# A transformer block kernel on one core: the token factor of three norms moved from the products' input to their results, and one unused group of products left out

## The chip, the cores and the metric

The kernel is one program on one core of one Trainium2 chip. The metric is the time of one execution on the device, in microseconds (us). The core has a matrix engine (TensorE, PE in the profile; its weight loads are listed apart as PEld), VectorE (DVE), ScalarE (ACT), GpSimd (POOL) and SyncE (SP), which here only issues transfers. Each engine works through its own list of instructions in order, and the lists meet only at semaphores. Matmul results go to eight banks of PSUM (`pb0` to `pb7`, 128 x 512 floats each), from where DVE or ACT must fetch them before the bank is used again.

## The reference, cut to what matters

Two blocks follow each other over 512 tokens of 1024 features, all in float32. The change is in the second one:

```python
def rms_norm(x, w):
    xf = x.astype(jnp.float32)
    y = xf * lax.rsqrt(jnp.mean(xf * xf, axis=-1, keepdims=True) + EPS)
    return (y * w.astype(jnp.float32)).astype(x.dtype)

def swiglu(x, w_gate, w_up, w_down):
    return (jax.nn.silu(x @ w_gate) * (x @ w_up)) @ w_down

def second_block(x, ...):
    x = x + 0.5 * swiglu(rms_norm(x, ffn1_norm[l]), ffn1_w_gate[l], ffn1_w_up[l], ffn1_w_down[l])
    h = rms_norm(x, mix_norm[l])
    proj = h @ w_in[l]
    qkv_a, z_a, a_a, b_a, qkv_b = jnp.split(proj, split_at, axis=-1)
    o_a = gdn_mixer(qkv_a, z_a, a_a, b_a, conv_w[l], a_log[l], dt_bias[l], gdn_norm_w[l])
    o_b = dilated_mixer(qkv_b, q_norm_w[l], k_norm_w[l], rel_bias)
    x = x + jnp.concatenate([o_a, o_b], axis=-1) @ w_out[l]
    x = x + 0.5 * swiglu(rms_norm(x, ffn2_norm[l]), ffn2_w_gate[l], ffn2_w_up[l], ffn2_w_down[l])
    x = rms_norm(x, final_norm[l])
```

A root-mean-square norm multiplies each feature by a weight and each token by one factor, 1/sqrt(mean of squares + EPS). That factor is the same for all features of the token, so it may also be multiplied onto a product's result.

## The kernel before, in words

Activations lie with features across the 128 partitions and the 512 tokens along them, as eight tiles of 128 x 512 (`KC` = 8) in `xT`. A group of products is eight matmuls of 128 x 128 weights with these eight tiles, summed in one bank. Weights of 1 MB (`pair`, two groups) are streamed by SP into a ring of three slots (L400); PE signals `slot_free` when it begins a slot.

A norm (`rms`, numbered 0 to 3) goes over four engines. ACT squares the tiles (L1276), DVE adds the squares (`add_square`, L1820, 128 x 512 each), PE sums them over the partitions by one matmul with ones (L852), DVE scales and adds EPS (L1824), ACT takes the root (L1278), DVE the reciprocal (L1826); the result `rs` holds the token's factor in every partition. Then DVE multiplies each tile by the weight and by `rs` in one instruction (L1829) and counts `xn_ready` up; the products of the next stage wait for tile after tile.

The feed-forward (`feed_forward`, twice) has 22 halves (`half`): 16 matmuls into two banks, gate and up (L863); ACT takes the Silu of the gate bank (L1283), DVE multiplies it by the up bank (L1834). Three pairs of banks take turns. Then eight groups of 22 matmuls go down (L888), and DVE adds half of each result to `xT` (L1848).

Between the two feed-forwards stand 30 groups (`linear`, L535, `N_H` = 30) that make queries, keys, values and gates of two attention parts, in two banks by turns. The 30th has the same weights as the 29th (gates) and nothing reads it. ACT copies each result out of its bank (L1299). Beside this, DVE runs a convolution of five taps over 12 of the groups (`convolve`, L1870 and four of L1875), ACT takes its Silu (L1303), and the first 16 groups are normed by head: ACT squares (L1309), PE sums (L907), DVE scales (L1904), ACT takes the root of eight sums at once (L1313), DVE the reciprocal and the multiplication (`apply_norm`, L1886, L1890). The groups of values (16 to 19) are convolved in the turns 16 to 19. Behind the groups a short chain over DVE (from L1910), ACT and PE prepares the gates; then come 32 heads of attention, the chunked recurrence, the output product (`project`, L1066; DVE adds it to `xT`, L2072), norm 2 and the second feed-forward, and norm 3, whose result is stored.

While norm 0 begins, POOL still scales and shifts the token-major copy of the first block's result, tile by tile (`scale_rows`, L432 and L434). The order of all work is the order in which the code lists it; no scheduler moves anything.

## Time and profile before

| | us |
|---|---|
| median of 3 runs | 3819.41 (3816.04 to 3820.52) |
| profiled execution, its own time | 3819.16 |
| its span | 3817.6 |
| PE busy | 3498.3 (92%) |
| DVE, ACT, POOL busy | 1159.3, 757.9, 177.0 |
| granted PE clock, mean | 0.95 of full |

The second block begins at about 2204 us of the span. A row of the timeline gives the start and the duration in us, engine, line, operation and tiles; in brackets stands the idle time of the engine ahead of it and who ended it. The granted clock 1.00 is 2.4 GHz and 0.50 is 1.2 GHz. Matmuls in float32 leave two records each and are pipelined, so a row with x160 is 80 matmuls.

### The profile page before, as it was taken

How to read it: one execution, taken by the hardware profiler on the slowest of the kernel's cores; microseconds unless marked ns; L12 is line 12 of the kernel's file. 1: busy time of each engine (PE TensorE's matmuls, PEld its weight loads, DVE VectorE, ACT ScalarE, POOL GpSimd, SP SyncE). 2: the span in 40 equal slices, each digit the busy share in tenths (PEclk: the TensorE clock that was granted, in tenths of full speed). 3: DMA queues.
4: the chain of work that ended last, by engine and by line, in shares of the span. 5: the costliest groups of instructions: out<-in, count | busy, mean ns of one | idle time of the engine just before them, and what ended most of it. 6: DMA issues, size and time to landing. Idle time of an engine off the chain costs nothing. (4 is left out here: it accounts for less than half of the span.)

```text
span 3817.6 us, 47479 instructions
## 1 busy us (share of the span) xinstructions
PE 3498.3 (92%) x15780; PEld 1803.3 (47%) x15780; DVE 1159.3 (30%) x2400; ACT 757.9 (20%) x1418; POOL 177.0 (5%) x169
## 2 busy tenths in 40 slices
PE   8998998899969989997999679999998788899998
PEld 5445444555544454445555334444344577444443
DVE  1564112322333751113332320000446555410001
ACT  1134112223221151102222220000123422100000
POOL 1000002100020000003000110000000000000000
PEclk9999999899979999998999889999999887999999
DMA  7112223898231103234986212235121000122221
GB/s 280 56 45 78 77 77 132 324 389 353 77 130 66 56 23 112 76 133 153 420 336 268 81 57 77 77 83 143 67 76 54 1 0 0 44 77 77 77 77 66
DMA packets 79142, 457.64 MB, mean 120 GB/s; under 512 B 12160, under 2 KB 12296, under 8 KB 32112
## 3 DMA queue, kind: packets, MB, share of 16 engines
q1 hardware_dynamic: 42912, 310.40, 21.6%
q0 software_dynamic: 19776, 112.50, 8.3%
q10 hardware_dynamic: 16272, 32.43, 2.5%
q8 instruction: 100, 1.64, 0.2%
q14 instruction: 82, 0.67, 0.1%
HBM read 416.23 MB, written 39.06 MB: 119 GB/s over the span
## 5 line engine op out<-in xcount | busy, mean ns | idle before, releaser
L779 PE MATMUL pb<-arena,xT 128*64 x1984 | 445.6, 383 | 16.4 <-DVE streamed L1699 5.9
L779 PE MATMUL pb<-streamed,xT 128*64 128x256 f32 x1984 | 445.6, 383 | 0.0
L535 PE MATMUL pb<-xT,streamed 128*128 128x512 f32 x832 | 369.4, 603 | 0.0
L779 PEld LDWEIGHTS pb<-arena,xT 128*64 128x64 f32 x1984 | 267.8, 138 | 162.4 <-issue 31.6
L704 PE MATMUL pb<-xT,streamed 128*128 128x512 f32 x768 | 335.3, 595 | 2.6 <-ACT arena L1193 2.6
L888 PE MATMUL pb<-arena,streamed 128*128 128x512 f32 x704 | 306.4, 598 | 8.9 <-DMA streamed<-in_w_tail 7.2
L863 PE MATMUL pb<-xtok,streamed 128*128 128x512 f32 x704 | 305.0, 596 | 5.8 <-DVE xtok L1829 5.8
L863 PE MATMUL pb<-arena,streamed 128*128 128x512 f32 x704 | 304.2, 595 | 5.8 <-DVE arena L1829 5.8
L779 PEld LDWEIGHTS pb<-streamed,xT 128*64 128x64 f32 x1984 | 267.9, 138 | 0.0
L535 PEld LDWEIGHTS pb<-xT,streamed 128*128 128x128 f32 x832 | 159.9, 193 | 201.5 <-issue 201.4
L704 PEld LDWEIGHTS pb<-xT,streamed 128*128 128x128 f32 x768 | 146.4, 191 | 186.6 <-issue 186.6
L803 PE MATMUL pb<-arena,am 128*64 x496 | 224.6, 595 | 5.7 <-DVE streamed L1745 5.7
L803 PE MATMUL pb<-streamed,am 128*64 128x512 f32 x496 | 224.6, 595 | 0.0
L888 PEld LDWEIGHTS pb<-arena,streamed 128*128 128x128 f32 x704 | 134.7, 192 | 180.7 <-issue 171.8
L863 PEld LDWEIGHTS pb<-xtok,streamed 128*128 128x128 f32 x704 | 134.6, 191 | 176.1 <-issue 174.6
L863 PEld LDWEIGHTS pb<-arena,streamed 128*128 128x128 f32 x704 | 134.4, 191 | 176.3 <-issue 175.0
L535 PE MATMUL pb<-xtok,streamed 128*128 128x512 f32 x480 | 211.8, 599 | 5.8 <-DVE xtok L1829 5.8
L1834 DVE TENSOR_TENSOR arena<-pb,arena 128x512 f32 (+1 forms) x44 | 30.4, 692 | 572.5 <-ACT arena L1283 572.5
L714 PE MATMUL pb<-arena,streamed 128*128 x384 | 168.7, 592 | 0.0
L1571 DVE TENSOR_TENSOR arena<-pb,arena 128x512 f32<-128x512 f32 x48 | 33.2, 692 | 421.3 <-PE pb L714 421.3
L535 PEld LDWEIGHTS pb<-xtok,streamed 128*128 128x128 f32 x480 | 92.2, 192 | 122.8 <-issue 121.2
L1215 ACT ACTIVATE streamed<-arena 128x2048 f32 x62 | 118.5, 1912 | 155.2 <-issue 121.9
(359 smaller groups left out, 3756.8 us busy)
## 6 DMA issues: line engine op xcount, KB each, us to landing
arena<-in_w_moe SPq DMA_DIRECT2D x128, 1024.0 KB, 11.7
streamed<-in_w_tail SPq DMA_DIRECT2D x87, 1024.0 KB, 4.8
streamed<-in_w_layer SPq DMA_DIRECT2D x78, 1024.0 KB, 4.9
arena<-in_w_moe POOLq DMA_DIRECT2D x64, 1024.0 KB, 9.7
ys_dram<-am ACTq DMA_DIRECT2D x120, 128.0 KB, 6.5
xT<-xs_dram ACTq DMA_DIRECT2D x26, 512.0 KB, 8.2
xs_dram<-lnw POOLq DMA_DIRECT2D x16, 512.0 KB, 20.5
lnw<-in_ln_par POOLq DMA_DIRECT2D x4, 1024.0 KB, 5.3
```

What stands on the lines that cost most here:

```text
L535: last = mm(pb[bank][:, 0:cols], unit(w, u, k), rhs[:, k * cols:(k + 1) * cols], start=(k == 0), stop=(k == KC - 1))
L704: last = mm(pb[2 + d % 2][:], unit(w, u6 % 2, k), grp(xT, k), start=(k == 0), stop=(k == KC - 1))
L714: last = mm(pb[4 + e][:], unit(w, ub % 2, e * 4 + k), grp(big, n * 4 + k), start=(k == 0), stop=(k == 3))
L779: last = mm(pb[m][r0:r0 + MOE_BLOCK, 0:FW], rows, w, start=(k == 0), stop=(k == KC - 1))
L803: last = mm(pb[2 + b % 2][r0:r0 + MOE_BLOCK, 0:DW], hT[:, h0:h0 + MOE_BLOCK], w, start=(k == 0), stop=(k == 3))
L863: last = mm(pb[3 * u + s][:], unit(w, u, k), xn[:, k * S:(k + 1) * S], start=(k == 0), stop=(k == KC - 1))
L888: last = mm(pb[6 + g][:], unit(w, u % 2, c % KC), grp(big, c), start=(c == 0), stop=(c == FC - 1))
L1215: fn(cut(w1_relay, D_EXP - FW), cut(arena[:, bass.ds(values[0], KC * D_EXP)], D_EXP)[:, :, FW:D_EXP], ACT.Copy).then_inc(w1_relayed, 1)
L1571: v.tensor_tensor(tmp[d % 2], pb[4 + d % 2][:], relu2[d % 2], ALU.mult).then_inc(br_free, 1)
L1834: v.tensor_tensor(grp(big, f), pb[3 + s][:], sgl[s], ALU.mult).then_inc(ff_free, 1)
```

## The change

The weighting by the norm's weight (`weigh`) and the token's factor (`row_scale`) become two functions for the norms 0, 1 and 2; norm 3 stays as it was. The products read tiles that are only weighted. For norm 0 the weighings stand ahead of the adds of squares; for the norms 1 and 2 each tile is weighed as soon as its sum is in `xT`. PE's matmul of the sum stands behind the first half of products or the first group. The factor is multiplied in elsewhere: onto the gate bank, into `sgl`, ahead of the Silu; onto the down products' results, together with the 0.5; and onto each result of the 29 groups, where DVE takes over the fetching from PSUM that was ACT's. The input of the second feed-forward lies in `sr` and no more in `xtok`. The four groups of values are convolved in the turns 18, 20, 22 and 24 (`V_AT`), and the last eight `apply_norm` of DVE stand one in each turn from 21 on in place of behind the loop.

```diff
-H_Q, H_K, H_SQ, H_SK, H_V, H_Z, H_SV, H_AB, N_H = 0, 4, 8, 12, 16, 20, 24, 28, 30
+H_Q, H_K, H_SQ, H_SK, H_V, H_Z, H_SV, H_AB, N_H = 0, 4, 8, 12, 16, 20, 24, 28, 29
+V_AT = [18, 20, 22, 24]
...
-        xns = [sr[:, 0:KC * S], xtok[:, :], xtok[:, :], xtok[:, :]]
+        xns = [sr[:, 0:KC * S], xtok[:, :], sr[:, 0:KC * S], xtok[:, :]]
... (tensor engine)
                 half(pair(j0), 0, 0, True)
+                rms(2 * n)
...
-            rms(0)
             feed_forward(0, 0)
-            rms(1)
             pe.wait_ge(rel_copied, 2)
             for g in range(N_H):
                 linear(pair(34 + g // 2), g % 2, xns[1], DEPTH * LIN_LAYER + g, g % 2, norm=1 if g == 0 else None)
+                if g == 0:
+                    rms(1)
...
-            rms(2)
             feed_forward(1, 53)
... (scalar engine)
-                    act.wait_ge(ff_ready, n * FC + f + 1)
-                    fn(sgl[s], pb[s][:], ACT.Silu).then_inc(ff_silu, 1)
+                    act.wait_ge(ff_scaled, n * FC + f + 1)
+                    fn(sgl[s], sgl[s], ACT.Silu).then_inc(ff_silu, 1)
...
-                act.wait_ge(lin_ready, DEPTH * LIN_LAYER + g + 1)
-                fn(grp(big, g), pb[g % 2][:], ACT.Copy).then_inc(lin_free, 1)
-                if g - 2 in CONV_GROUPS:
-                    c = CONV_GROUPS.index(g - 2)
+                done = g - 2 if g - 2 < H_SQ else H_V + V_AT.index(g - 2) if g - 2 in V_AT else -1
+                if done >= 0:
+                    c = CONV_GROUPS.index(done)
                     act.wait_ge(conv_ready, c + 1)
-                    fn(grp(big, g - 2), ctmp[c % 2], ACT.Silu).then_inc(conv_silu, 1)
+                    fn(grp(big, done), ctmp[c % 2], ACT.Silu).then_inc(conv_silu, 1)
                 c = g - 3
                 if 0 <= c < N_NORM:
+                    act.wait_ge(lin_free, DEPTH * LIN_LAYER + c + 1 + 2)
... (vector engine)
+            def weigh(m, k):
+                v.tensor_scalar(grp(xns[m], k), grp(xT, k), normw[:, m * KC + k:m * KC + k + 1], None, ALU.mult).then_inc(xn_ready, 1)
+            def row_scale(m):
                 dve.wait_ge(ss_ready, m + 1)
                 v.tensor_scalar(rs, pb[7][:], 1.0 / D, EPS, ALU.mult, ALU.add).then_inc(rvar, 1)
                 dve.wait_ge(rstd, m + 1)
                 v.reciprocal(rs, rs)
                 dve.drain()
...
                 def half(f, s):
+                    dve.wait_ge(ff_ready, n * FC + f + 1)
+                    v.tensor_tensor(sgl[s], pb[s][:], rs, ALU.mult).then_inc(ff_scaled, 1)
                     dve.wait_ge(ff_silu, n * FC + f + 1)
                     v.tensor_tensor(grp(big, f), pb[3 + s][:], sgl[s], ALU.mult).then_inc(ff_free, 1)
...
-                    x = grp(xT, d)
-                    v.scalar_tensor_tensor(out=x, in0=pb[6 + d % 2][:], scalar=0.5, in1=x, op0=ALU.mult, op1=ALU.add).then_inc(dn_free, 1)
+                    x, y = grp(xT, d), sgl[d % 3]
+                    v.scalar_tensor_tensor(out=y, in0=pb[6 + d % 2][:], scalar=0.5, in1=rs, op0=ALU.mult, op1=ALU.mult)
+                    dve.drain()
+                    v.tensor_tensor(x, x, y, ALU.add).then_inc(dn_free, 1)
+                    if n == 0:
+                        dve.drain()
+                        weigh(1, d)
...
+            dve.drain()
+            for k in range(KC):
+                weigh(0, k)
             for k in range(KC):
                 add_square(0, k)
-            rms(0)
+            row_scale(0)
...
-            for g in range(N_NORM + 5):
-                if g in CONV_GROUPS:
+            for g in range(N_H):
+                dve.wait_ge(lin_ready, DEPTH * LIN_LAYER + g + 1)
+                v.tensor_tensor(grp(big, g), pb[g % 2][:], rs, ALU.mult).then_inc(lin_free, 1)
+                dve.drain()
+                if g < H_SQ:
                     convolve(g)
+                elif g in V_AT:
+                    convolve(H_V + V_AT.index(g))
...
-            for c in range(8):
-                apply_norm(1, c)
-            dve.drain()
+                if g >= N_NORM + 5:
+                    apply_norm(1, g - N_NORM - 5)
+                    dve.drain()
...
                 v.tensor_tensor(x, x, pb[OUT_BANKS[d]][:], ALU.add).then_inc(lin_free, 1)
+                dve.drain()
+                weigh(2, d)
```

On PE, where the first block ends and the second begins, the list before reads so (L548 are the last transposes, L852 the matmul of the sum, L863 the first half of products; x7 means seven alike):

```order
L548 MATMUL pb3<-cst,xtok 128x128 x4
L590 REGISTER_ALU
L590 COMPARE_AND_BRANCH
L852 MATMUL pb7<-am,cst 128x512 [waits squares_summed,xT_rest,xT_ready]
L863 MATMUL pb0<-arena,streamed 128x512 [waits xn_ready,ff_free,weights_loaded0]
L863 MATMUL pb0<-arena,streamed 128x512 [waits xn_ready] x7
L863 MATMUL pb3<-arena,streamed 128x512 x8
L869 UNCONDITIONAL_BRANCH
```

And now, at the same place (L854 is the matmul of the sum, L865 the products):

```order
L592 REGISTER_ALU
L592 COMPARE_AND_BRANCH
L865 MATMUL pb0<-arena,streamed 128x512 [waits ff_free,weights_loaded0,xn_ready,xT_rest,xT_ready]
L865 MATMUL pb0<-arena,streamed 128x512 [waits xn_ready] x7
L865 MATMUL pb3<-arena,streamed 128x512 x8
L854 MATMUL pb7<-am,cst 128x512 [waits squares_summed]
L872 UNCONDITIONAL_BRANCH
```

The matmul of the sum has moved behind the sixteen products of the first half.

On DVE, at the same place, before (L1820 the adds, L1824 and L1826 the factor, L1829 the input):

```order
L1820 TENSOR_TENSOR am<-am,arena 128x512 [waits sq_ready,xT_ready]
L1820 TENSOR_TENSOR am<-am,arena 128x512 [waits sq_ready] x6
L1824 TENSOR_SCALAR arena<-pb7 128x512 [waits sums_ready]
L1826 RECIPROCAL arena<-arena 128x512 [waits rms_std]
L1829 SCALAR_TENSOR_TENSOR arena<-xT,normw,arena 128x512 x8
L1836 UNCONDITIONAL_BRANCH [waits rows_scaled]
```

And now (L1826 is the weighing, L1822 the adds, L1831 and L1833 the factor, L1845 the new scaling of a gate bank):

```order
L1826 TENSOR_SCALAR arena<-xT,normw 128x512 [waits xT_ready]
L1826 TENSOR_SCALAR arena<-xT,normw 128x512 x7
L1822 TENSOR_TENSOR am<-am,arena 128x512 [waits sq_ready] x7
L1831 TENSOR_SCALAR arena<-pb7 128x512 [waits sums_ready]
L1833 RECIPROCAL arena<-arena 128x512 [waits rms_std]
L1849 UNCONDITIONAL_BRANCH [waits rows_scaled]
L1849 ISA
L1845 TENSOR_TENSOR arena<-pb0,arena 128x512 [waits ff_ready]
```

Eight instructions that waited for the factor became eight ahead of the adds that wait only for `xT`.

On DVE in the groups, where one turn has both a convolution and a norm by head, before (L1870 and L1875 the convolution, L1886 and L1890 `apply_norm`, L1904 the next sum):

```order
L1870 TENSOR_SCALAR arena<-arena,conv_w 128x512 [waits conv_silu,lin_free]
L1875 SCALAR_TENSOR_TENSOR arena<-arena,conv_w 128x510
L1875 SCALAR_TENSOR_TENSOR arena<-arena,conv_w 128x511 x2
L1875 SCALAR_TENSOR_TENSOR arena<-arena,conv_w 128x510
L1886 RECIPROCAL am<-am 128x512
L1890 SCALAR_TENSOR_TENSOR arena<-arena,am 128x512
L1904 TENSOR_SCALAR am<-pb 128x512 [waits norm_sums]
```

And now, in turn 18 and at the start of turn 19 (L1917 fetches a result from PSUM, L1890 and L1895 are the convolution, L1906 and L1910 `apply_norm`, L1929 the next sum):

```order
L1917 TENSOR_TENSOR arena<-pb,arena 128x512 [waits lin_ready]
L1890 TENSOR_SCALAR arena<-arena,conv_w 128x512 [waits conv_silu]
L1895 SCALAR_TENSOR_TENSOR arena<-arena,conv_w 128x510
L1895 SCALAR_TENSOR_TENSOR arena<-arena,conv_w 128x511 x2
L1895 SCALAR_TENSOR_TENSOR arena<-arena,conv_w 128x510
L1906 RECIPROCAL am<-am 128x512
L1910 SCALAR_TENSOR_TENSOR arena<-arena,am 128x512
L1929 TENSOR_SCALAR am<-pb 128x512 [waits norm_sums]
L1917 TENSOR_TENSOR arena<-pb,arena 128x512 [waits lin_ready]
```

The fetch that frees PE's bank stands in DVE's list now, behind all that the turn before had to do.

## Rows read from the trace of the kernel before

**Rows 1.** The page, part 1: engine, busy us (share), instructions.
```profile
PE 3498.3 (92%) x15780; PEld 1803.3 (47%) x15780; DVE 1159.3 (30%) x2400; ACT 757.9 (20%) x1418; POOL 177.0 (5%) x169
```
**Rows 2.** Waits of PE from 2224 us on: total us, times, longest.
```profile
PE pb L852 <- DVE am L1820: 7.7, 3, 2.8
...
PE pb L535 <- DVE xtok L1829: 5.8, 1, 5.8
```
**Rows 3.** Timeline of norm one: start us, duration us, engine, line.
```profile
2202.76 1.37 DVE L1456 TENSOR_SCALAR xT<-pb,ln_T 128x128 f32<-128x128 f32 x4 [3.95 <-PE pb L548]
...
2216.43 2.05 PE L852 MATMUL pb<-am,cst 128*128 128x512 f32 x2 [14.07 <-DVE am L1820]
...
2223.33 5.39 DVE L1829 SCALAR_TENSOR_TENSOR arena<-xT,normw,arena 128x512 f32<-128x512 f32 x8
...
2224.23 20.99 PE L863 MATMUL pb<-arena,streamed 128*128 128x512 f32 x44 [5.75 <-DVE arena L1829]
...
2240.10 0.60 ACT L1283 ACTIVATE arena<-pb 128x512 f32<-128x512 f32 x1 [18.93 <-PE pb L863]
```
**Rows 4.** DVE's adds (ns, min/median/max) and POOL's last two scalings beside them.
```profile
L1820 DVE TENSOR_TENSOR am<-am,arena x7: 692/693/2661, 2206.0 to 2215.6; 128x512 f32<-128x512 f32 x7
...
2207.05 2.80 POOL L432 TENSOR_TENSOR xtok<-xtok,lnw 128x1024 f32<-128x1024 f32 x1
...
2209.99 2.61 POOL L434 TENSOR_TENSOR xtok<-xtok,lnw 128x1024 f32<-128x1024 f32 x1
```
**Rows 5.** Groups of instructions by line: busy us, mean ns.
```profile
L1834 DVE TENSOR_TENSOR arena<-pb,arena 128x512 f32 (+1 forms) x44 | 30.4, 692 | 572.5 <-ACT arena L1283 572.5
...
L1870 DVE TENSOR_SCALAR arena<-arena,conv_w 128x512 f32<-128x512 f32 x12 | 5.8, 484 | 33.2 <-ACT arena L1303 20.8 <-ACT arena L1299 12.4
```
**Rows 6.** Timeline of norm two.
```profile
2694.00 0.69 DVE L1848 SCALAR_TENSOR_TENSOR xT<-pb,xT 128x512 f32<-128x512 f32 x1 [17.41 <-PE pb L888]
...
2703.26 27.26 PE L535 MATMUL pb<-xtok,streamed 128*128 128x512 f32 x56 [5.76 <-DVE xtok L1829]
```
**Rows 7.** Stages: window, its length, PE, PEld, DVE, ACT, POOL busy, clock, DMA.
```profile
2533.50:2535.00 1.50, 1.50 (x3) 0.68 (x2) 0.00 (x0) 0.00 (x0) 0.99 (x1) 0.50 0.29 38
...
2708.50:2709.40 0.90, 0.90 (x3) 0.41 (x2) 0.00 (x0) 0.00 (x0) 0.00 (x0) 0.57 1.03 437
...
3346.00:3347.60 1.60, 1.60 (x4) 0.57 (x3) 0.82 (x2) 0.00 (x0) 0.00 (x0) 0.51 0.81 323
...
3647.20:3649.00 1.80, 0.10 (x1) 0.00 (x0) 0.69 (x1) 1.65 (x2) 0.00 (x0) 1.00 0.00 0
```
**Rows 8.** Timeline of the groups: DVE's steps, then PE's, then what follows them.
```profile
2757.52 0.49 DVE L1870 TENSOR_SCALAR arena<-arena,conv_w 128x512 f32<-128x512 f32 x1 [3.34 <-ACT arena L1303]
...
2761.23 0.69 DVE L1904 TENSOR_SCALAR am<-pb 128x512 f32<-128x512 f32 x1
...
2816.65 3.35 DVE L1886 RECIPROCAL am<-am 128x512 f32<-128x512 f32 x1 [20.17 <-ACT am L1313]
...
2821.46 3.34 DVE L1886 RECIPROCAL am<-am 128x512 f32<-128x512 f32 x1
...
2787.86 7.03 PE L535 MATMUL pb<-xtok,streamed 128*128 128x512 f32 x16
...
2795.59 7.03 PE L535 MATMUL pb<-xtok,streamed 128*128 128x512 f32 x16
...
2857.39 68.83 PE L535 MATMUL pb<-xtok,streamed 128*128 128x512 f32 x160
...
2928.06 0.29 DVE L1910 COPY ab<-pb 128x128 f32<-128x128 f32 x1 [17.62 <-PE pb L913]
```
**Rows 9.** Timeline of norm three.
```profile
3333.08 0.69 DVE L2072 TENSOR_TENSOR xT<-xT,pb 128x512 f32<-128x512 f32 x1 [1.96 <-PE pb L1066]
...
3342.32 17.86 PE L863 MATMUL pb<-xtok,streamed 128*128 128x512 f32 x35 [5.75 <-DVE xtok L1829]
```
**Rows 10.** Timeline at the end of the first feed-forward's halves.
```profile
2529.88 1.88 PE L877 MATMUL pb<-arena,rel_b 32*8 32x512 f32 x4 [1.41 <-DVE arena L1834]
```

More of the change, by code:

```diff
@@ L292, in two_blocks @@
             sem(n) for n in ("sq_ready", "sq_used", "squares_summed", "sums_ready", "rms_var", "rms_std", "xn_ready"))
-        ff_ready, ff_silu, ff_free = sem("ff_ready"), sem("ff_silu"), sem("ff_free")
+        ff_ready, ff_scaled, ff_silu, ff_free = sem("ff_ready"), sem("ff_scaled"), sem("ff_silu"), sem("ff_free")
         dn_ready, dn_free = sem("down_ready"), sem("down_free")
@@ L1820, in add_square @@
                     v.tensor_tensor(sq_sum, sq_sum, sq2[k % 2], ALU.add).then_inc(sq_summed if k == KC - 1 else sq_used, 1)
-            def rms(m):
+            def weigh(m, k):
+                v.tensor_scalar(grp(xns[m], k), grp(xT, k), normw[:, m * KC + k:m * KC + k + 1], None, ALU.mult).then_inc(xn_ready, 1)
+            def row_scale(m):
                 dve.wait_ge(ss_ready, m + 1)
@@ L1827, in rms @@
                 dve.drain()
+            def rms(m):
+                row_scale(m)
                 for k in range(KC):
@@ L1853, in _ @@
             dve.wait_ge(xT_ready, 4 * KC + 1)
+            dve.drain()
+            for k in range(KC):
+                weigh(0, k)
             for k in range(KC):
                 add_square(0, k)
-            rms(0)
+            row_scale(0)
             dve.wait_ge(tok_done, 2 * DEPTH + 1)
             feed_forward(0)
-            rms(1)
+            row_scale(1)
             dve.wait_ge(rel_stored, 16)
@@ L1865, in convolve @@
                 x, y = grp(big, g), ctmp[c % 2]
-                dve.wait_ge(lin_free, DEPTH * LIN_LAYER + g + 1 + 2)
                 if c >= 2:
@@ L1892, in apply_norm @@
                     last.then_inc(n_done, 1)
-            for g in range(N_NORM + 5):
-                if g in CONV_GROUPS:
+            for g in range(N_H):
[3 more added lines that the diff above has]
+                if g < H_SQ:
                     convolve(g)
+                elif g in V_AT:
+                    convolve(H_V + V_AT.index(g))
                 c = g - 5
-                if c >= 0:
+                if 0 <= c < N_NORM:
                     if c >= 8:
@@ L2075, in _ @@
             add_square(2, KC - 1)
-            rms(2)
+            row_scale(2)
             feed_forward(1)
```

## The prediction

> **What bounds the kernel now.** I read the page first: TensorE (PE) is busy for 92% of the span [rows 1], so time can only be taken out of matmuls, out of the gaps between them, or out of stretches in which its clock is low. I then read the table of waits for the part behind the first 2224 us [rows 2] and looked up its large entries in the timeline: the three norms that the change touches are gaps in which PE waits for a chain on VectorE (DVE) and ScalarE (ACT). Last I read the same stretches in the table of stages, for the granted clock. I call the norms one (ahead of the first feed-forward), two (ahead of the 30 groups of products) and three (ahead of the second feed-forward). All three are short, so everything below is worked out from starts and ends in the timeline.
>
> In norm one the input is whole at 2204.13 (DVE L1456 from 2202.76 for 1.37), the sum of squares goes to PE at 2216.43, and the first product starts at 2224.23 [rows 3]. In norm two the last product is taken from PSUM at 2694.00 and the next one starts at 2703.26 [rows 6]; in norm three it is 3333.08 and 3342.32 [rows 9]. Now the products need only the weighted input (x times the norm's weight). The factor of the token, rs, is needed where a result leaves PSUM.
>
> **Units.** A group of eight matmuls takes 6.87 us at full clock (160 records, two a matmul, in 68.83 us), so one matmul 0.86; two products' starts lie 7.73 apart where one matmul of a sum stands between them [rows 8], which is 6.87 + 0.86 again. A DVE instruction with 512 columns from PSUM takes 0.69, the same times one number a row from SBUF to SBUF 0.48 [rows 5]; a drain adds about 0.08 (the step of 4.81 below holds instructions of 3.35, 0.69 and 0.69, together 4.73).
>
> **Norm one.** Eight weighings now stand ahead of the adds of squares. If nothing held them, the first would end at about 2204.9 and PE start there, 19.3 us earlier; in that place GpSimd (POOL) still runs its row scaling, until 2209.99 + 2.61 = 2212.60. The adds of before show what this does: their median is 693 ns, the longest took 2661 ns, and between two POOL instructions just one of them came through [rows 4]. No weighing ran beside POOL before, so its cost is unknown: between 0.48, as alone, and one for each POOL instruction, as the adds. I take the second: at 0.48 against 0.69 it moves elements faster than an add does, so it uses at least as much of the way to SBUF. Then weighings end at about 2205.0, 2207.7, 2210.4 and 2213.1, and the other four by 2214.7; PE does three matmuls in the holes and goes on without a stop from 2213.15. Thirteen of the half's sixteen matmuls are left, 11.2 us, and 2.0 to 2.8 more at low clock (below): it ends at 2226.4 to 2227.1. The seven adds, 0.78 each, end by 2220.2, so the matmul of the sum follows at once, 0.86, and the second half starts at about 2227.6. Before, it started with ACT's first Silu, 2240.0 [rows 3]. **Minus 12.4**; if nothing holds the weighings, minus 18.0 (first half 2205.0 to 2221.1, sum to 2222.0).
>
> The Trainium skill bears on the choice. Its page SBUF — State Buffer, section Who interferes with whom, says that GpSimd and VectorE share a pair of SBUF ports under an exclusive lock, taken for a whole instruction, by VectorE instructions with two SBUF inputs and also by tensor_scalar in its two-port mode; the trace agrees for the first kind, with the 2661 ns, and shows nothing of the second. By that rule the term is the minus 12.4, and by the reading that a single tensor input stays clear of POOL it is the minus 18.0.
>
> The old chain, matmul of the sum to first product (2216.43 + 2.05 to 2223.33 + 0.75, so 4.9 us until rs is there and 0.75 for a multiplication), now runs beside the second half of products. The first result waits for it until about 2232.6, which costs nothing: three pairs of banks are free, and the fourth half starts at 2227.6 + 27.5 = 2255.
>
> **Ends of both feed-forwards.** 22 halves of 13.7 us each get one more DVE multiplication (0.69 and about 0.06 to hand over), hidden but for the last, where PE waits for the chain Silu, multiplication [rows 10]: now scaling, Silu, multiplication. **Plus 0.75, twice.** The downward products get a second instruction and drain a group (0.77), hidden under 18.9 us but at the last: at the end of the first it is part of norm two, at the end of the kernel **plus 0.77**.
>
> **Norm two.** Last product out at 2694.00, 0.69, drain, add 0.69 to 2695.46, and PE goes on at about 2695.6: the weighings 0 to 6 are long done, and the eighth (0.5 more) is needed only 6 us later. **Minus 7.7**. The matmul of the sum no longer stands in a gap: **plus 0.86**.
>
> **The clock.** After each of the old gaps the granted clock was 0.5 (1.2 GHz of 2.4) for some microseconds: until 2708.8 and until 3347.6 [rows 7]. By the sum, norm two's groups cost 2926.22 - 2703.26 = 222.96 where 30 x 6.87 + 16 x 0.86 = 219.8 were due: 3.2 us; norm three likewise 2.8. The gaps shrink from 2.4 + 5.8 us to 1.8 and 0.9. In the gap of 1.7 us at the end of the second feed-forward, and behind it, the clock stayed at 1.0; behind the like gap of the first (1.4 us, then two short matmuls that use eight columns of the array) a stretch from 2533.5 stood at 0.5 [rows 7]. I take no fall: **minus 3.2 and minus 2.8**. If it falls after all, between 0 and 2.8 comes back at a place; I price it at two thirds of norm three's, 1.9, since the gaps are shorter.
>
> **The groups.** Group 30, which nothing reads, goes: **minus 6.87** on PE. ACT's copy out of PSUM becomes a DVE multiplication. Is DVE in time? Steps from starts in rows 8: a convolution 2761.23 - 2757.52 = 3.71; reciprocal, multiplication and the next sum's scaling 2821.46 - 2816.65 = 4.81; the new copy 0.77. So the turns are 0.77 + 3.71 (groups 0 to 7, and + 0.61 from 5), 0.77 + 4.81 = 5.58 (13 to 20) and, with one of the four convolutions (18, 20), 9.29; from 21 on 0.77 + 4.19, and 8.67 at 22 and 24. PE needs 7.73 a group until 19, 6.87 after. A copy may begin up to 5.9 us late before PE waits for its bank. Turn by turn DVE is 1.6 late at 19, 2.4 at 21, there also held by the square root of 4096 columns, 3.8 at 22, 5.6 at 23, 3.7, 5.5, 3.6, 1.7, and on time at 28. At the start rs is there 13.5 us behind the first product, bank 0 is wanted at 14.6. So no wait, by 0.3 us; I put it at **0**, bounds 0 to 2.
>
> Behind the groups PE ends at 2695.6 + 0.86 + 29 x 6.87 + 16 x 0.86 = 2909.4. The short chain for the gates (DVE L1910) began 1.84 behind PE's end [rows 8]. It now stands behind the last copy and the last reciprocal, 0.2 + 0.77 + 4.19 = 5.2: **plus 3.35**. Before, those reciprocals ran ahead of PE's end; here is what the change gives back.
>
> **Norm three.** Last addition 3333.08 to 3333.77, then PE at 3333.9 in place of 3342.32: **minus 8.4**, and **plus 0.86** for the sum's matmul. POOL does no arithmetic here or in norm two.
>
> **Sum.** -12.4 + 0.75 - 7.7 + 0.86 - 3.2 - 6.87 + 3.35 - 8.4 + 0.86 - 2.8 + 0.75 + 0.77 = -34.0. The profiled execution took 3819.2 us (span 3817.6), so 3785.1; it lies 0.25 below the median, so **3785.4**. Its own range is 3781 to 3790: 0 to 2 for the bank wait, 1 for hand-overs, and 2 to 3 because the phase in which the clock falls in the recurrence (about 3000 to 3270) may come out otherwise.
>
> **Rivals.**
> - The weighings are not held by POOL: 5.6 more, **3779.8**. For it: no row shows the form held. Against: the adds were.
> - The clock falls after the short gaps too, at norms two and three, and at the second feed-forward's end, whose gap grows from 1.7 to 2.5: 3 x 1.9 = 5.7, and with 2 of bank waits **3793**. For it: the 0.5 at 2533.5. Against: the 1.0 at 3647.2 [rows 7].
> - VectorE becomes the bound of the groups, and it ends slower: where a copy is later than 5.9 us PE waits, and if the clock falls at each wait, that costs at the old rate (norm three) 2.8 a group. From 13 late groups on (34.0 / 2.8 = 12.1) all is lost; with 14 it is 3785.4 + 39 = **3824**. For it: margins of 0.3 and 0.4 at groups 23 and 25. Against: DVE has 99 us of work in groups 13 to 28 (16 x 0.77 + 4 x 3.71 + 8 x 4.81 + 8 x 4.19) and PE 116, so DVE would have to be half slower than its rows.
> - It does not free PE as it says: the start in norm one is tied to the end of the row scaling as a whole, so that the first weighing comes at 2212.6 and the first product at 2213.2. That is 11.0 earlier, less 0.86 for the sum's matmul: 10.1 in place of 12.4, and **3787.7**. For it: only one instruction at a time came through beside POOL. Against: one did come through each time.
>
> **How the numbers follow.** Forecast 0.55; unheld 0.13; falling clock 0.19; other tie 0.08; slower 0.03; 0.02 for unforeseen smaller gains that end near no change. The range 3776 to 3796 takes in the first four with 2 to 4 us at each end. What a measurement here can tell from no change is about 0.2%, 7.6 us; faster by more 0.95, within 0.02, slower 0.03.
>
> **What would show it.** In the new trace: PE's second half of products starting at about 2227 to 2228, and single weighings of some 2.6 us beside POOL's; the first group's product about 12.4 - 0.75 + 7.7 = 19.4 us earlier than 2703.26 and at clock 1.0; no wait of a group's product for the new copy of more than 2 us in all; DVE L1910's counterpart 5 us behind the last group; norm three's gap below 1 us. Wrong would be: first product near 2205 with weighings of 0.48 in a row, or waits for the copies in every group.

## The result and the profile after

The changed kernel takes 3793.3 us, median of four runs (3790.7 to 3796.7), beside 3819.6 for the kernel before; the ratio is 0.9933 with a 95% interval of 0.9916 to 0.9951. That is 26.3 us less, where 34.0 was forecast. It lies inside the stated range (3776 to 3796), but outside the sum's own (3781 to 3790), and nearest to the 3793 of the rival with the falling clock. The profiled execution was the slowest of the four (3796.7, span 3795.0), so the two traces differ by 22.6 us only. The two should be kept apart: terms are read in the traces, the gain is the difference of medians.

TensorE's busy time has hardly moved against [rows 1], though a whole group of matmuls is gone. The page of the changed kernel:

```profile
PE 3504.2 (92%) x15764; PEld 1810.0 (48%) x15764; DVE 1217.9 (32%) x2489; ACT 742.8 (20%) x1389; POOL 176.4 (5%) x169
```

Less work in more time means that somewhere the same matmuls ran slower. The waits that the change was about are gone or small. TensorE's waits from 2200 us on (total us, times, longest), to be held against [rows 2]:

```profile
PE pb L891 <- DMA streamed<-in_w_tail: 9.5, 2, 5.4
PE pb L927 <- DVE ga L1951: 9.0, 1, 9.0
...
PE pb L865 <- DVE arena L1826: 3.9, 4, 2.7
...
PE pb L854 <- DVE am L1822: 3.2, 1, 3.2
...
PE pb L537 <- DVE xT L1863: 1.6, 1, 1.6
...
PE pb L916 <- DVE arena L1917: 1.0, 1, 1.0
...
PE pb L865 <- DVE xT L2097: 0.8, 1, 0.8
```

No copy out of a bank (L1917) makes a group wait, apart from the 1.0 at the start of the gates' chain.

Norm one in the changed kernel's timeline, as [rows 3, 4]:

```profile
2199.89 9.53 DVE L1826 TENSOR_SCALAR arena<-xT,normw 128x512 f32<-128x512 f32 x8 [0.35 <-ACT xT L1127]
...
2200.19 2.40 POOL L436 TENSOR_TENSOR xtok<-xtok,lnw 128x1024 f32<-128x1024 f32 x1
2200.53 2.05 PE L865 MATMUL pb<-arena,streamed 128*128 128x512 f32 x2 [2.75 <-DVE arena L1826]
...
2202.55 2.52 POOL L434 TENSOR_TENSOR xtok<-xtok,lnw 128x1024 f32<-128x1024 f32 x1
2202.93 2.07 PE L865 MATMUL pb<-arena,streamed 128*128 128x512 f32 x2 [0.35 <-DVE arena L1826]
...
2207.90 13.55 PE L865 MATMUL pb<-arena,streamed 128*128 128x512 f32 x26 [0.41 <-DVE arena L1826]
...
2221.28 1.02 PE L854 MATMUL pb<-am,cst 128*128 128x512 f32 x2
2222.14 8.32 PE L865 MATMUL pb<-arena,streamed 128*128 128x512 f32 x19
```

One weighing comes through for each of GpSimd's scalings, and with it one matmul (two records); once GpSimd is done the rest runs without a hole. The weighings' own durations (ns, min/median/max) say the same:

```profile
L1826 DVE TENSOR_SCALAR arena<-xT,normw x8: 473/481/2577, 2199.9 to 2208.9; 128x512 f32<-128x512 f32 x8
```

Norms two and three, and the clock behind them (timeline and stages of the changed kernel), against [rows 6, 7, 9]:

```profile
2682.91 7.13 PE L537 MATMUL pb<-xtok,streamed 128*128 128x512 f32 x16 [1.55 <-DVE xT L1863]
...
3320.32 14.00 PE L865 MATMUL pb<-arena,streamed 128*128 128x512 f32 x32 [0.78 <-DVE xT L2097]
```
```profile
2683.00:2688.00 5.00, 5.00 (x12) 2.30 (x13) 1.83 (x3) 0.52 (x1) 0.00 (x0) 1.00 0.55 184
3320.00:3325.00 5.00, 4.68 (x11) 2.20 (x12) 2.13 (x4) 0.63 (x1) 0.00 (x0) 1.00 0.47 152
```

The ends of the two halves of the work, against [rows 10, 8]: the gap behind the first feed-forward's halves is 2.17 and not 1.41, the 9 groups from 20 on stand without a stop, and the gates' first copy comes 5.3 us behind their end. From the timeline of the changed kernel:

```profile
2512.87 1.88 PE L880 MATMUL pb<-arena,rel_b 32*8 32x512 f32 x4 [2.17 <-DVE arena L1847]
...
2834.94 61.96 PE L537 MATMUL pb<-xtok,streamed 128*128 128x512 f32 x144
...
2902.25 0.29 DVE L1935 COPY ab<-pb 128x128 f32<-128x128 f32 x1
```

**Where the 22.6 us are.** Each row of this table runs from one start or end in the two timelines to the next; all stretches together make the two spans.

| stretch | before | after | difference | forecast |
|---|---|---|---|---|
| start to input of norm one whole | 2204.4 | 2199.8 | -4.6 | 0 |
| to first downward product | 327.3 | 314.9 | -12.4 | -11.65 |
| first downward products | 162.3 | 166.7 | +4.4 | 0 |
| norm two's gap | 9.30 | 1.55 | -7.75 | -7.7 |
| groups | 222.96 | 213.99 | -8.97 | -9.2 |
| to the gates' first copy | 1.84 | 5.34 | +3.5 | +3.35 |
| attention | 73.5 | 74.65 | +1.2 | 0 |
| recurrence | 307.5 | 318.6 | +11.1 | 0 |
| rest of its output products | 24.00 | 24.00 | 0 | 0 |
| norm three's gap | 9.28 | 0.78 | -8.5 | -8.4 |
| second feed-forward, halves | 306.7 | 305.7 | -1.0 | -1.2 |
| its downward products | 151.33 | 151.33 | 0 | 0 |
| end | 17.24 | 17.62 | +0.4 | +0.8 |

The rows that the change touches come to -34.8 beside a forecast of -34.0. The rest, +12.1, is in stretches whose instructions on TensorE are the same, the recurrence above all. The row "recurrence" runs to the first addition of its output to `xT`, and so holds the first output products, 31.1 us in both traces; the difference lies ahead of them. Its two rows in the tables of stages (window, its length, PE, PEld, DVE, ACT, POOL busy, clock, DMA), of before and then of after:

```profile
3001.53:3309.04 307.51, 252.45 (x3249) 204.40 (x3250) 160.88 (x438) 70.82 (x212) 0.00 (x0) 0.82 0.03 9
```
```profile
2976.90:3295.54 318.64, 267.04 (x3249) 217.19 (x3250) 161.18 (x438) 70.54 (x212) 0.00 (x0) 0.76 0.03 8
```

Both have 3249 matmul records; TensorE is busy 14.6 us longer, at a mean granted clock of 0.76 in place of 0.82. The experiments ask whether that belongs to the change.

### The profile page after: what moved, and what is told of

It reads as the page before. It is cut to its first block and busy times, and to the rows that moved or that the text cites. A ratio compares the mean times of both kernels' runs of the same rounds, so it can differ in the third digit from the quotient of the medians.

```text
span 3795.0 us, 47563 instructions
## 1 busy us (share of the span) xinstructions
PE 3504.2 (92%) x15764; PEld 1810.0 (48%) x15764; DVE 1217.9 (32%) x2489; ACT 742.8 (20%) x1389; POOL 176.4 (5%) x169
## 5 line engine op out<-in xcount | busy, mean ns | idle before, releaser
L865 PE MATMUL pb<-arena,streamed 128*128 128x512 f32 x1408 | 610.9, 596 | 4.7 <-DVE arena L1826 3.9
L865 PEld LDWEIGHTS pb<-arena,streamed 128*128 128x128 f32 x1408 | 268.5, 191 | 346.3 <-issue 334.9
L891 PE MATMUL pb<-arena,streamed 128*128 128x512 f32 x704 | 308.5, 601 | 12.0 <-DMA streamed<-in_w_tail 9.5
L891 PEld LDWEIGHTS pb<-arena,streamed 128*128 128x128 f32 x704 | 135.5, 193 | 185.0 <-issue 173.8
L537 PE MATMUL pb<-xtok,streamed 128*128 128x512 f32 x464 | 202.2, 592 | 1.6 <-DVE xT L1863 1.6
L1845 DVE TENSOR_TENSOR arena<-pb,arena 128x512 f32<-128x512 f32 x44 | 30.4, 692 | 475.3 <-PE pb L865 474.8
L1573 DVE TENSOR_TENSOR arena<-pb,arena 128x512 f32<-128x512 f32 x48 | 33.2, 692 | 419.7 <-PE pb L716 419.7
L537 PEld LDWEIGHTS pb<-xtok,streamed 128*128 128x128 f32 x464 | 88.0, 190 | 113.0 <-issue 110.4
L1701 DVE COPY streamed<-arena 128x2048 f32 x62 | 76.1, 1227 | 179.6 <-DMA arena<-in_w_moe 87.6
L1285 ACT ACTIVATE arena<-arena 128x512 f32<-128x512 f32 x44 | 27.7, 629 | 530.9 <-DVE arena L1845 530.9
```

Of the source, the lines that this page charges most:

```text
L537: last = mm(pb[bank][:, 0:cols], unit(w, u, k), rhs[:, k * cols:(k + 1) * cols], start=(k == 0), stop=(k == KC - 1))
L865: last = mm(pb[3 * u + s][:], unit(w, u, k), xn[:, k * S:(k + 1) * S], start=(k == 0), stop=(k == KC - 1))
L891: last = mm(pb[6 + g][:], unit(w, u % 2, c % KC), grp(big, c), start=(c == 0), stop=(c == FC - 1))
L1701: v.tensor_copy(cut(w3_relay, D_EXP - FW), cut(arena[:, bass.ds(values[0] + 2 * PAIR, KC * D_EXP)], D_EXP)[:, :, FW:D_EXP]).then_inc(w3_re ...
```

## The experiments

All were timed in the same job as runs of the kernel before, whose median was 3822.5, 3820.6 and 3821.9 in the three jobs. A table of stretches for all profiles follows the last one.

**The changed kernel again (e1_again).** No edit.

> The changed kernel once more, unaltered. Its profiled execution kept 22.6 us of the span where the terms of the sum that could be read at their places come to 34; the rest went in the stretch of the downward products (4.4 us) and in the recurrence (341.0 us from the last matmul ahead of it to the first output product's addition, where the kernel before took 329.9). Theory: the 11 us of the recurrence are the phase of its granted clock, which differs from one execution to the next; then the same stretch comes out otherwise here, somewhere from 330 to 341 us, and the median of the times stays at 3793. Rival: the changed kernel has a slower recurrence for good; then it is 341 again, within 1 us. The two waits for weights in the downward products (5.45 and 4.07 us) should come again within 1 us by either.

Measured: 3794.4 (3788.9 to 3800.2, six runs), ratio 0.9923 [0.9905, 0.9941]. The recurrence took 318.3 us, as the rival said. The waits for weights were 4.97 and 2.10, so the second, 4.07 in the first profile, did not come again within 1 us, as was expected by either, and the downward products took 161.8 in place of 166.7. One part of the loss was chance; the other needed more kernels.

**Only the thirtieth group left out (e2_group30).**

```
 # kernel before
-H_AB, N_H = ..., 28, 30
+H_AB, N_H = ..., 28, 29
```

> The kernel before with the thirtieth group of products left out, which nothing reads, and nothing else. By its eight matmuls 6.87 us go from TensorE: 3819.6 - 6.9 = 3812.7. Rival: another chain ended the stretch (the copies and the norms on VectorE), and the time stays within 2 us of 3819.6.

Measured: 3821.9 (12 runs), ratio 1.0000 [0.9988, 1.0012]: no gain to be seen, and the interval leaves room for 4.6 us at most, so the 6.9 of the forecast missed. In the trace the groups took 216.10 in place of 222.96, the 6.87 of the forecast. But the recurrence took 314.3 in place of 307.5. So the rival's reason (another chain ends the groups) is wrong, though the time stayed as it said, and a term can be read in its place and still be missing from the median. Where it went is open; the recurrence is one candidate (see below).

**The weighings of norm one on ScalarE (e3_weigh_act).**

```
 # dve: "for k in range(KC): weigh(0, k)" taken out
 # act, ahead of rms(0):
+act.drain()
+for k in range(KC):
+    fn(grp(xns[0], k), grp(xT, k), ACT.Copy, scale=normw[:, k:k + 1]).then_inc(xn_ready, 1)
```

> The changed kernel with the eight weighings of norm one made by ScalarE ahead of its squares. Theory (VectorE's weighings are held one by one by GpSimd's row scaling, ScalarE's are not): the eight run without a hole at some 0.62 us each, the first half of products has no hole, and its sum's matmul and the second half come 13.7 + 0.9 us behind the first product, 2215 to 2217 on the clock of the changed kernel's trace, in place of 2222.1: 5 us less, 3788. Rival: GpSimd slows every engine's way to SBUF, or the low granted clock behind the long gap makes the holes, not the lock: then the weighings of ScalarE take over 1 us or the first half lasts 20 us as now, and the time stays at 3793.

Measured: 3789.5, ratio 0.9912 [0.9894, 0.9929]. Its timeline:

```profile
2198.99 5.01 ACT L1296 ACTIVATE arena<-xT,normw 128x512 f32<-128x512 f32 x8
...
2199.86 16.73 PE L865 MATMUL pb<-arena,streamed 128*128 128x512 f32 x32 [2.98 <-ACT arena L1296]
...
2201.58 2.35 POOL L434 TENSOR_TENSOR xtok<-xtok,lnw 128x1024 f32<-128x1024 f32 x1
...
2216.42 1.02 PE L854 MATMUL pb<-am,cst 128*128 128x512 f32 x2
```

Eight weighings in 5.01 us while GpSimd scales, and 16 matmuls without a hole. Of the two, only VectorE is held. The sum's matmul comes 17.5 us behind the input (2198.89), where it came 21.5 and 20.0 behind it in the two profiles of the changed kernel. At the first downward product 1.3 to 3.4 us are left of that (311.5 us against 312.8 to 314.9 in the others with the changed code): the term is a quarter to two thirds of the 5 that the theory gave it. The theory had priced the 16 matmuls at full clock, 13.7 us; they took 16.73, with a granted clock of 0.50 until 2204.9. The median's 4.9 against the changed kernel's in the same job holds some chance.

**The gates' chain ahead of the last norm (e4_gates_first).**

```
-if g >= N_NORM + 5:
+if N_NORM + 5 <= g < N_H - 1:
     apply_norm(1, g - N_NORM - 5)
...
 v.tensor_tensor(cut(ga[:, :], UN), ..., ALU.max).then_inc(ab_ready, 1)
+apply_norm(1, 7)
 dve.wait_ge(sp_ready, 1)
```

> The changed kernel with the last of the eight reciprocals and multiplications of the keys' norm moved behind the start of the chain for the gates. Theory (VectorE's last norm stands ahead of the gates' chain and TensorE waits for that chain): the chain starts 1.0 us behind TensorE's last group in place of 5.2, so 4.2 us less, 3789. Rival: the chain's later links, on ScalarE, wait for the norm or for something else anyway, and the time stays at 3793.

Measured: 3786.8, ratio 0.9905 [0.9887, 0.9924]. From TensorE's last group to the first copy of the gates it is 2.20 us in place of 5.34: 3.1 back, as against the 3.5 that the change had lost there. It is not 4.2, since the copy of the last group and the gates' transposes stay in the way. The median fell by 7.6 against the changed kernel's in the same job, more than the term: the recurrence took 308.8 in this profile, against 318.3 in that one.

**Half the recurrence, before and after (e5_before_short, e6_after_short).** Both have the same edit, which leaves out four of the eight chunks and with them half of the results.

```
+RNC = 4
-with pe.Fori(0, NCH // 2 - 1) as i:      # also act, dve
+with pe.Fori(0, RNC // 2 - 1) as i:
-chunk(NCH - 2, 0, True); chunk(NCH - 1, 1, False)
+chunk(RNC - 2, 0, True); chunk(RNC - 1, 1, False)
```

> The kernel before with four of the recurrence's eight chunks left out (and so half of its results missing). It is the base for the changed kernel cut in the same way. The stretch from the start of the recurrence to its output products took 307.5 us for eight chunks in the trace of before; with four it should take about half, 150 to 160 us, and the time be near 3667. Six profiles so far had 307.5 to 318.6 us for that stretch, whose code none of them changed, with 54.6 to 76.8 us of clock lost in it. Theory (phase of the granted clock): with half the chunks the scatter from run to run is halved too. Rival: the scatter comes from elsewhere, and stays.

> The changed kernel with the same four chunks of the recurrence left out. The terms read at their places come to 33.6 us (12.4 from the input to the first downward product, 7.75, 8.97 less 3.5 less 1.2, 8.5, 1.0, less 0.4), and the downward stretch gives back 0 to 4.4. Theory (what was missing from the forecast was lost in the recurrence by the phase of its clock): against the kernel before with the same cut it is 30 to 34 us faster. Rival: the change costs 8 us somewhere whatever the recurrence does; then the difference is 26 us, as for the whole kernels.

Measured: 3698.6 and 3661.3; ratios to the full kernel before 0.9682 [0.9669, 0.9695] and 0.9570 [0.9554, 0.9585]. The medians differ by 37.3 us, more than either theory said. With five runs each this is known to some 8 us only. The profiled execution before was the fastest of its five and the one after the fourth of its five, and their spans differ by 29.1 us. So the medians speak against 26, and the traces' spans do not. In the traces the stretches that the change touches differ by 36.2 us: the gaps of norm two and of norm one's input to the first downward product give 8.7 and 13.7, a little more than in the first pair. But the scatter was not halved (3691 to 3703, and 3649 to 3663), and the short recurrences still differ, 179.8 and 186.9 us, at clocks 0.83 and 0.76. So some scatter comes from elsewhere, and the recurrence of the changed kernel was again the slower one.

**The convolutions late (e7_late_conv).**

```
-V_AT = [18, 20, 22, 24]
+V_AT = [20, 21, 22, 23]
```

> The changed kernel with the four convolutions of the value groups in the turns of groups 20 to 23 in place of 18, 20, 22 and 24, which is the order that loads VectorE most. It tests the rule by which no wait was forecast: a copy may begin up to 5.9 us late before TensorE waits for its bank. By the rows, VectorE is 2.4 us late at group 21, there held 3.3 more by the square root of 4096 columns, and then 1.8 more for each turn of 8.67: TensorE waits 1.6, 1.8 and 1.8 us for the copies, 5.2 in all, and the stretch of the groups is 219.2 us long in place of 214.0, the time 3799. Rival (VectorE the bound, the clock falls at every wait): the same waits with 2 to 3 us more for each, 225 us or more for the stretch and 3805 or more. Other rival: the rule is too strict and nothing happens, 214.0.

Measured: 3795.2, ratio 0.9936 [0.9921, 0.9950]; the groups took 216.5 us, 2.5 more. Its PE timeline:

```profile
2829.97 34.50 PE L537 MATMUL pb<-xtok,streamed 128*128 128x512 f32 x80
2864.90 7.11 PE L537 MATMUL pb<-xtok,streamed 128*128 128x512 f32 x16 [0.43 <-DVE arena L1917]
2873.64 20.84 PE L537 MATMUL pb<-xtok,streamed 128*128 128x512 f32 x48 [1.63 <-DVE arena L1917]
```

Group 20 starts at 2829.97 and ends at 2836.8, so group 23 ends at 2857.4 and its copy was due then; VectorE began it at 2864.07, 6.6 late, and TensorE waited, 0.43; for the next one 1.63. The 2.1 us of waits are what the groups lost, give or take 0.5; the rule holds within that, and the clock did not fall. My sum was too high because it added the square root's hold (3.08 us in the changed kernel) to a queue that is late already: here the square root is done before VectorE gets there.

**Both improvements (e8_both).** The edits of e3_weigh_act and e4_gates_first together.

> The changed kernel with both improvements: the weighings of norm one on ScalarE (it took 4.6 us from the start of the second half of products, 3.8 us off the median) and the last reciprocal and multiplication of the norm behind the start of the gates' chain (3.15 us off the chain, 6.5 off the median, of which more than half would be the recurrence's phase). If both terms add, 3793.9 - 4.0 - 3.2 = 3786.7; by the medians of the two alone 3783.5. Rival: one of them was the phase alone, and the time is 3790.

Measured: 3792.5, ratio 0.9919 [0.9906, 0.9932]. Both terms are in the trace (311.5 us from input to the first downward product, 2.20 to the gates' copy), 4.4 to 6.5 us less together than in the profiles with the changed kernel's own code there; and the recurrence took 320.2 us, the slowest of all. By its rows this is the best version, by its time it can't be told from the changed kernel.

**The kernel before again (e9_before_again).** No edit.

> The kernel before once more, unaltered, for a second look at its recurrence, which took 307.5 us in the first. In the profiles of the kernels whose other code is that of the changed one it took 318.6, 318.3, 312.3, 308.8, 318.8 and 320.2, and 314.3 where only the thirtieth group was left out of the kernel before. Theory (it differs from one execution to the next, with the phase of the granted clock): anything from 307 to 320, and all other stretches as in the first profile within 1 us, but for the two around the store of the position table. Rival (the kernel before has a fast recurrence for good): 307.5 within 1.

Measured: 3817.5 (11 runs) beside 3821.9 for the same kernel in the same job, ratio 0.9993 [0.9984, 1.0002]. Two medians of one kernel differ by 4.4 us. The recurrence took 310.7, so it is not fixed to within 1 us, as the rival had it. Not all else was the same within 1 us: the input of norm one was whole 3.1 us earlier.

**The same with a few matmuls more (e10_group30_4, e11_after_2, e12_after_5).** A shift of the start of all that follows; e10 on the kernel of e2_group30 with 4, the others on the changed kernel with 2 and 5.

```
 def linear(..., again=0):
     pe.wait_ge(lin_free, n + 1)
+    for _ in range(again):
+        mm(pb[bank][:, 0:cols], unit(w, u, 0), rhs[:, 0:cols], start=True, stop=True)
 linear(..., again=N if g == 6 else 0)
```

> The kernel before without the thirtieth group, and with four matmuls of group 6 made once more (3.4 us of TensorE, the clock at full speed there), which alters nothing but when the rest begins. Without the four the stretches it touches were 6.9 us shorter, and still the median was 3821.9 beside 3822.5. Theory (the recurrence's loss follows where its start falls against the fall of the clock, and the start has a usual place in each kernel): the median is not 3.4 above 3821.9, but between 3815 and 3822. Rival (the missing 6.9 is plain scatter, or something fixed that came with the missing group): 3.4 above the kernel without the group, 3817 to 3825, no more telling than that; only a median below 3819 or above 3828 would tell.

> The changed kernel with two matmuls of group 6 made once more, 1.7 us of TensorE. Everything behind starts 1.7 us later. Theory (phase): the recurrence, 318.6 and 318.3 us in two profiles of the changed kernel, comes out elsewhere between 307 and 320, and the median may be below that of the changed kernel (3793.9) in spite of the added work. Rival (no phase; a fixed slower recurrence): 318.5 within 1, and 3795.6.

> The changed kernel with five matmuls of group 6 made once more, 4.3 us. Theory (phase): as for two matmuls, a recurrence between 307 and 320 us that does not go with the added work, and a median up to 11 us off 3798.2. Rival: 318.5 us, and 3798.2. In both, group 6 takes 4.3 us more and VectorE, which is early there, hides none of it.

Measured: 3822.3, 3790.3 and 3794.5; ratios 1.0000 [0.9990, 1.0010], 0.9923 [0.9910, 0.9937] and 0.9926 [0.9913, 0.9939]. The recurrences took 316.4, 311.5 and 317.9, and the groups of the last two 1.7 and 4.3 us more, as the added matmuls should. The stage row of the changed kernel with 2 more:

```profile
2970.45:3281.95 311.50, 258.42 (x3249) 209.92 (x3250) 161.12 (x439) 70.57 (x212) 0.00 (x0) 0.80 0.03 8
```

The fixed recurrence of 318.5 us is refuted: 311.5 in code that differs by two matmuls 250 us earlier, and 308.8 and 312.3 in e4 and e3. That the start of the recurrence decides, and each kernel has its usual place, is not shown: 317.9 agrees with the rival's 318.5 within 1, one kernel's own runs scatter by 11 us (3788.9 to 3800.2), and e10's result fits both.

All full kernels, us. "Input" is when norm one's input is whole, "down" the first downward products.

| profile | input | down | recurrence | its clock | median |
|---|---|---|---|---|---|
| before | 2204.4 | 162.3 | 307.5 | 0.82 | 3819.6 |
| e9 (before) | 2201.3 | 160.7 | 310.7 | 0.80 | 3817.5 |
| e2 (no group 30) | 2197.6 | 161.4 | 314.3 | 0.79 | 3821.9 |
| e10 (the same, 4 more) | 2202.6 | 161.3 | 316.4 | 0.78 | 3822.3 |
| after | 2199.8 | 166.7 | 318.6 | 0.76 | 3793.3 |
| e1 (after) | 2203.3 | 161.8 | 318.3 | 0.77 | 3794.4 |
| e3 | 2198.9 | 164.8 | 312.3 | 0.80 | 3789.5 |
| e4 | 2205.0 | 166.9 | 308.8 | 0.82 | 3786.8 |
| e7 | 2196.9 | 166.7 | 318.8 | 0.76 | 3795.2 |
| e8 | 2205.3 | 163.2 | 320.2 | 0.75 | 3792.5 |
| e11 (after, 2 more) | 2197.6 | 162.0 | 311.5 | 0.80 | 3790.3 |
| e12 (after, 5 more) | 2200.3 | 161.7 | 317.9 | 0.77 | 3794.5 |

## Why the prediction came out as it did

**The mechanism was right, and nearly all signed terms with it.** Norm one: the weighings are held one by one, with a longest of 2577 ns where 2.6 us was forecast; the second half starts 22.4 us behind the input, where 23.5 was forecast, partly because GpSimd had 7.8 us left to run and not 8.2. (The prediction put the whole input at 2204.13, where VectorE's last part ends; ScalarE's last part of `xT` ended at 2204.37, which changes no term by more than 0.24.) In the six other profiles that weigh on VectorE the second half started 20.2 to 21.2 us behind the input. The step "I take the second" is confirmed from both sides, by the 2577 and by e3_weigh_act, whose ScalarE form is not held. The rule of the Trainium skill's page SBUF — State Buffer, section Who interferes with whom, that tensor_scalar in its two-port mode takes the shared lock too, agrees with this.

**The gaps** of norms two and three fell to 1.55 and 0.78 us, and the clock did not fall behind them: 1.00 in both stage rows. All nine profiles with the changed code, the shortened one among them, show no low clock from there to the end of the groups, or in norm three, and the second feed-forward's downward products took 151.33 us in all fourteen. So the rival with the falling clock is out at its three places; that its 3793 is the measured time is chance. At a fourth place the clock did fall, and there the first profile misleads: behind the first feed-forward's halves the clock was low in all five profiles of the old code (gap 1.41 us), and in six of the nine of the new (gap 2.17), though not in the first. Timeline and stage of e1_again:

```profile
2516.91 39.49 PE L891 MATMUL pb<-arena,streamed 128*128 128x512 f32 x88
...
2602.91 75.80 PE L891 MATMUL pb<-arena,streamed 128*128 128x512 f32 x176 [2.10 <-DMA streamed<-in_w_tail]
```
```profile
2517.00:2520.00 3.00, 3.00 (x4) 1.40 (x5) 1.28 (x2) 0.00 (x0) 1.11 (x1) 0.52 0.00 0
```

**VectorE is in time**, as worked out turn by turn, with nothing to spare. The copy of group 23 starts at 2868.32, with the group's end at 2862.4: 5.9 us late, where 5.6 was forecast and 5.9 allowed. e7_late_conv shows what is behind that edge: 2.5 us for two waits and no fall of the clock, so the rival "VectorE the bound" had the price per late group (2.8 us) too high by more than half.

**The gates' chain** cost 3.5 (3.35 forecast), and e4_gates_first gives 3.1 back.

**The start tied to the whole row scaling** is out: the first matmul started at 2200.53, 7 us ahead of GpSimd's end.

**What failed is the sum's treatment of the stretches that are not changed.** The prediction gave the recurrence "2 to 3" us in the range for its clock, and the first downward products nothing. That the time still lies in the stated range is owed to the 2 to 4 us added at each end, and in part to luck: the first pair of profiles lost 15.5 us there, and 34.0 less 15.5 would have been 3801.

- Recurrence. The same 3249 matmul records took 307.5 to 320.2 us in twelve profiles, with the granted clock between 0.82 and 0.75. That is the largest term of the difference between the two traces, 11.1 us, and it was not in the sum. The profile that I built on was the fastest of the four with the old code (mean 312.2; the eight with the new code 315.8), so the difference that can be expected is 3.6 rather than 11. Whether even this 3.6 belongs to the change is not settled: the two sets overlap (307.5 to 316.4, and 308.8 to 320.2), but the shortened pair leans the same way by 7. A rival divides the same twelve profiles otherwise, by the thirtieth group: with it 307.5 and 310.7 (mean 309.1), without it the ten others, 308.8 to 320.2 (mean 315.7). By this, leaving the group out would cost the recurrence 6.6 us, about what it gains ahead, which fits the median of e2_group30. No run shows why it should, two profiles are few, and the changed kernel with the group put back was not run; it stays open.
- First downward products. The weights' stream shares the DMA engines with the 4 MB store of the position table there, and TensorE waits for weights twice in both kernels. Timelines of before and of after:

```profile
2531.69 39.73 PE L888 MATMUL pb<-arena,streamed 128*128 128x512 f32 x88
2576.50 39.54 PE L888 MATMUL pb<-arena,streamed 128*128 128x512 f32 x88 [5.08 <-DMA streamed<-in_w_tail]
2618.16 75.80 PE L888 MATMUL pb<-arena,streamed 128*128 128x512 f32 x176 [2.12 <-DMA streamed<-in_w_tail]
```
```profile
2514.68 38.03 PE L891 MATMUL pb<-arena,streamed 128*128 128x512 f32 x88
2558.16 40.80 PE L891 MATMUL pb<-arena,streamed 128*128 128x512 f32 x88 [5.45 <-DMA streamed<-in_w_tail]
2603.04 78.32 PE L891 MATMUL pb<-arena,streamed 128*128 128x512 f32 x176 [4.07 <-DMA streamed<-in_w_tail]
```

  The waits grew by 2.3 us, and the same 88 and 176 records took 3.8 us longer at a low clock behind them; what lies ahead of the first wait was 1.7 shorter, since the clock stayed up there (first row below). Stages ahead of the first wait of the changed kernel and behind both, and then behind the second of the kernel before:

```profile
2514.00:2552.00 38.00, 38.00 (x89) 16.64 (x88) 3.14 (x5) 0.63 (x1) 1.11 (x1) 1.00 0.60 109
2558.00:2565.00 7.00, 6.84 (x10) 3.00 (x11) 0.00 (x0) 0.00 (x0) 0.00 (x0) 0.59 0.73 171
2602.00:2609.00 7.00, 5.96 (x8) 2.56 (x9) 0.00 (x0) 0.00 (x0) 0.95 (x1) 0.56 0.55 195
```
```profile
2617.00:2624.00 7.00, 5.84 (x14) 2.73 (x15) 0.55 (x1) 0.43 (x1) 0.95 (x1) 1.00 0.69 221
```

  After the wait of 2.12 us the clock is 1.00, after the one of 4.07 it is low. Over all profiles the stretch is 161.5 us on average with the old code (five) and 163.9 with the new (nine): 2.4 given back. The new ones fall in two kinds: the three in which the clock stayed up at the start (after, e4, e7) took 166.7 to 166.9 us, with a second wait of 4.07 to 4.66 and a low clock behind it; the six in which it fell took 161.6 to 164.8, with a second wait of 1.57 to 2.95 and a clock of 1.00 behind it. The old ones are all of the second kind, 160.7 to 162.3. What ties the two places together was not tried. I had not looked at this stretch, though it lies between two of the norms. That the store is what delays the weights was read from the trace, and not tried by moving it.

**The sum over all profiles.** The touched stretches differ between profiles as well, so averages have to be set against averages. From the input to the first downward product it is 327.2 us on average in the five old ones and 313.6 in the seven new ones that weigh on VectorE: -13.7 in place of the first pair's -12.4. Norm two's gap was 9.30 in the first profile and 10.16 to 10.25 in the four other old ones, where the sum's matmul ran at low clock too (1.96 to 2.04 us in place of 1.10): -8.5 in place of -7.75. With the other rows the touched stretches come to -36.6, which the shortened pair's 36.2 agrees with. The recurrence gives back 3.6, the downward products 2.4 and the attention 0.8 (73.7 and 74.5 on average): -29.8. Over all runs of the two unaltered kernels, the medians are 3820.6 (66 runs) and 3794.1 (10), -26.5. The last 3.3 are not explained; two medians of one kernel differed by 4.4. By the rival of the thirtieth group, with 6.6 in place of 3.6, it would be -26.8.

## What to carry over

Read a change's terms at their places in the trace, and judge its gain by medians over many runs: here a term of 6.87 us stood in the trace to the hundredth and could not be seen in the median of 12 runs. Before summing, profile the kernel before several times and take the spread of each stretch as its noise (here two profiles of it differed by 3.2 us in the recurrence, and twelve of the same instructions by 12.7); a stretch with many short waits of TensorE needs bounds of its own, even if no instruction in it changes. A factor by token or by row can leave the path of a norm if it is applied behind the products, but look at who shares a way with the instruction that takes its place, and at what was early before and now stands in the queue (here the gates' chain).

## What the runs showed of the hardware

- Beside GpSimd's elementwise scaling (2.3 to 2.5 us each, 128x1024), a VectorE instruction with one tensor from SBUF and a number per row, 128x512, waits as long as one with two tensors: 2577 ns against 481 alone. ScalarE's, with the same operands, took 5.01 us for eight and was not held.
- TensorE's clock was 1.00 of 2.4 GHz behind idle gaps of 0.78 and 1.55 us, in every profile of the changed code, and 0.5 to 0.57 behind those of 5.75 [rows 7, 9]. Behind the waits of 5.45 and 4.07 us for weights it was low too, behind that of 2.12 it was not. The length of the gap does not settle it alone: behind the 1.41 us ahead of the first downward products it was 0.50 [rows 7], and behind the 2.17 us at the same place of the changed code 0.52 in one profile (e1_again) and 1.00 in another (the first).
- Where TensorE works in short bursts, as in the recurrence, its mean granted clock differed from 0.75 to 0.82 between executions of the same instructions, worth up to 12.7 us in 310.
